# Two buffers of an fp32 transformer kernel placed 64 bytes later in SBUF

## The reference, cut to what matters

```
y = modulate(rmsnorm(h, norm), shift, scale)
h = h + 0.5 * gate * swiglu(y, w_gu, w_down)      # six times: 1024 -> 2 x 2816 -> 1024
q, k, v, gu, gv = split(y @ w_in)                  # block 1: attention and gMLP, then w_out
q, k, v, u = split(y @ even_in)                    # block 2, layer 0: attention and Hyena
q, k, v, g = split(y @ ret_in)                     # block 2, layer 1: retention
shift, scale, gate = split(silu(c) @ w_ada + b)    # nine vectors of 1024 for each layer
```

## Time and profile before

| | |
|---|---|
| median of three runs | 2521.0 us |
| the profiled execution, its own time | 2521.01 us |
| its span | 2518.8 us |
| TensorE busy | 2441.2 us, 97% of the span |
| VectorE busy | 1515.7 us, 60% |
| ScalarE busy | 893.0 us, 35% |
| mean granted TensorE clock | 0.983 |

### The profile page before, as it was taken

How to read it: one execution, slowest core, us unless ns; L and a number is a source line. 1 busy time by engine, 2 the same in 40 slices (tenths; PEclk the granted TensorE clock), 3 DMA queues, 4 the chain that set the end, 5 groups by cost and what they waited for, 6 DMA issues and landing times.

```text
span 2518.8 us, 39335 instructions
## 1 busy us (share of the span) xinstructions
PE 2441.2 (97%) x14736; PEld 2153.7 (86%) x14736; DVE 1515.7 (60%) x2434; ACT 893.0 (35%) x1103; POOL 380.4 (15%) x353
## 2 busy tenths in 40 slices
PE   6998989999999998999999999999999999999999
PEld 4998879999888888867788888888888889999999
DVE  7676767977877665356478776642222365555444
ACT  4443454454222223432232222242222242244443
POOL 2110531211111102332211111001110001000110
PEclk7999989999999999999999999999999999999999
DMA  7778736854655554211135555522222242134455
GB/s 278 277 261 278 256 134 213 272 198 165 220 187 188 174 167 144 80 63 51 67 115 201 195 169 186 167 87 97 100 84 92 91 160 72 64 117 167 170 177 169
DMA packets 79878, 400.19 MB, mean 159 GB/s; under 512 B 8816, under 2 KB 12912, under 8 KB 54704
## 3 DMA queue, kind: packets, MB, share of 16 engines
q1 hardware_dynamic: 77216, 393.39, 45.1%
q0 software_dynamic: 1056, 3.67, 0.4%
q10 hardware_dynamic: 1520, 1.95, 0.2%
HBM read 396.88 MB, written 2.10 MB: 158 GB/s over the span
## 4 chain that ended last, share of the span: by engine, by line
PE 83%; DVE 8%; ACT 3%; DMA 3%; issue 2%; POOL 0%; ACTq 0%; SPq 0%; DVEq 0%; POOLq 0%
PE pg L1158 24%; PE pg L1160 23%; PE pg L1159 23%; DMA raw<-w_d 2%; PE pg L1334 2%; PE pg L1335 2%; PE pg L1336 2%; DVE wlo L2048 1%; PE px L1976 1%; DMA raw<-w_t 1%; ACT whi L661 1%; DVE ada L2088 1%; PE px L1737 1%; ACT whi L666 1%; PE pg L1776 1%
## 5 line engine op out<-in xcount | busy, mean ns | idle before, releaser
L1158 PE MATMUL pg<-Yh,whi 128*128 128x256 f32 (+1 forms) x2856 | 957.4, 335 | 28.5 <-DVE Yl L2208 7.7
L1159 PE MATMUL pg<-Yl,whi 128*128 128x256 f32 (+1 forms) x2856 | 946.9, 332 | 0.0
L1160 PE MATMUL pg<-Yh,wlo 128*128 128x256 f32 (+1 forms) x2856 | 946.8, 331 | 0.0
L2053 DVE TENSOR_TENSOR wlo<-raw,whi 128x2048 fp32r<-128x2048 f32 (+1 forms) x202 | 415.3, 2056 | 517.3 <-ACT whi L666 516.5
L1158 PEld LDWEIGHTS pg<-Yh,whi 128*128 128x128 f32 x2856 | 546.6, 191 | 91.5 <-issue 21.0
L1160 PEld LDWEIGHTS pg<-Yh,wlo 128*128 128x128 f32 x2856 | 546.5, 191 | 49.9
L1159 PEld LDWEIGHTS pg<-Yl,whi 128*128 128x128 f32 x2856 | 546.8, 191 | 49.2
L666 ACT ACTIVATE whi<-raw 128x2048 fp32r<-128x2048 f32 (+1 forms) x202 | 348.4, 1725 | 565.0 <-PE pg L1160 517.2
L1158 PE MATMUL pg<-Hh,whi 128*128 128x256 f32 (+1 forms) x1122 | 367.1, 327 | 7.0 <-DVE wlo L2053 4.5
L1160 PE MATMUL pg<-Hh,wlo 128*128 128x256 f32 (+1 forms) x1122 | 364.9, 325 | 0.0
L1159 PE MATMUL pg<-Hl,whi 128*128 128x256 f32 (+1 forms) x1122 | 364.8, 325 | 0.0
(11 more groups left out here) (352 smaller groups left out, 2361.7 us busy)
## 6 DMA issues: line engine op xcount, KB each, us to landing
raw<-w_t SPq DMA_DIRECT2D x194, 1024.0 KB, 5.0
ada<-w_ada SPq DMA_DIRECT2D x200, 512.0 KB, 3.6
raw<-w_d SPq DMA_DIRECT2D x96, 704.0 KB, 4.1
ADA<-w_ada SPq DMA_DIRECT2D x16, 512.0 KB, 14.0
NB<-na_bias POOLq DMA_DIRECT2D x8, 256.0 KB, 2.9
X<-x_t ACTq DMA_DIRECT2D x2, 512.0 KB, 16.4
spectrum<-HF POOLq DMA_DIRECT2D x1, 1024.0 KB, 11.1
X<-ctx_t SPq DMA_DIRECT2D x1, 1024.0 KB, 8.1
```

Of the source, the lines that this page charges most:

```text
L1158: pe.matmul(out, w_hi, y_hi, start=first, stop=False)
L1159: pe.matmul(out, w_hi, y_lo, start=False, stop=False)
L1160: return pe.matmul(out, w_lo, y_hi, start=False, stop=last)
L2053: dve.tensor_tensor(wlo[:, n % 2, 0:size], raw[:, n % 2, 0:size], whi[:, n % 2, 0:size].bitcast(F32), ALU.subtract)\
```

## The change

```
     X = sb("X", [P, KD, 512])
+    at[0] += 64
     y_at = at[0]
     Yh = sb("Yh", [P, 4096], F32R)
     Yl = sb("Yl", [P, 4096], F32R)
+    at[0] += 64
     raw = sb("raw", [P, 2, BLK])
     whi = sb("whi", [P, 2, BLK], F32R)
     wlo = sb("wlo", [P, 2, BLK], F32R)
```

## The result

The changed kernel takes 2531.1 us, the median of seven runs (2524.9 to 2539.7), against 2520.3 for the kernel before (seven runs, 2517.2 to 2526.8). The ratio is 1.0043, with a 95% interval from 1.0028 to 1.0057: 10.8 us slower, 7 to 14. I had forecast 4.6 us faster, and the time lies above the range.

The account below looks back on a forecast made before the run. TensorE's matmul pace was taken to bound the kernel, busy 97% of the span. Terms -22.1 (256 columns), +23.9 (512 columns) and -6.4 (Y stationary) sum to -4.6 us, 2521.0 to 2516.4 us; range 2512 to 2529.5.

Parts of the forecast that it names:

- its two signs: Matmuls over moving Y: 256 columns get 6.67 ns shorter, 22.1 us gained; 512 columns 6.67 ns longer, 23.9 us lost.
- the rule of even and odd by 128 bytes: All float32r products: paces are even multiples of 16 cycles where both operands' remainders by 128 agree, odd where they differ.
- D: Rival: the remainder is not the cause, H's pace comes from something else in its stages, nothing moves, 2521.0 us; chance 0.06.
- The 512-column term: Moving Y at 512 columns, mainly l0_gu1, l0_gu2 and l1_gu1: each matmul 6.67 ns longer, 23.9 us lost in all.
- I take from the H rows that a matmul of 256 columns over a moving Y gets 6.67 ns shorter: Moving Y at 256 columns: pace goes from 120.0 to 113.3 ns, 22.1 us gained after what is hidden.
- I count both stages in full: b1_gu1 and l1_gu2: weights keep up, so all 1056 matmuls in each count, 7.04 us each, 14.1 us gained together.
- the matmuls with Y stationary: 960 matmuls in l0_in and l1_in: one step of 6.67 ns each, taken as a gain of 6.4 us.
- B: Rival: only the moving operand's place counts, matmuls with Y stationary keep 120.0 ns, 2522.8 us; chance 0.26.
- C: Rival: a stationary operand off the 128-byte mark is dearer, 126.7 ns in l0_in and l1_in, 2529.2 us; chance 0.14.
- my terms for the 512-column matmuls in `l0_in` and `l1_in`: Moving Y at 512 columns, partly hidden: 2.8 us lost from l0_in to l0_out and 1.1 us in l1_in.
- The stretches that I had set to nothing: b1_down1, b1_down2 and l1_down2 at 0; in b1_in no product leads the chain, so no gain was taken.
- `b1_gu2`: 256 columns over Y: VectorE's loop of 5.72 us a block makes TensorE wait for wlo, gain 2.1 us instead of 7.04.

Follow-up runs that it names:

- e2: Kernel before with weights' parts whi and wlo 64 bytes later and H, behind them, 128 later, Y unmoved; 2527.9 us, ratio 1.0020.
- e1: Changed kernel with whi and wlo also 64 bytes later and all behind them 128 later, so Y, weights and H have remainder 64; 2533.5 us, ratio 1.0045.
- e13: Kernel before with weights 64 bytes later in l0_gu2 and, behind two blocks, in l0_gu1 and l1_gu1 (512 columns); 2541.6 us, ratio 1.0086.
- e9: Kernel before with weights 64 bytes later only in b1_gu1, b1_out, b1_gu2 and l1_gu2 (256 columns); 2509.0 us, ratio 0.9950.
- e14: Kernel before with weights 64 bytes later only in the value blocks, those with Y stationary; ratio 0.9993.
- e4: The changed kernel again, word for word, for a second trace; 2531.6 us, ratio 1.0036 against the kernel before.
- e3: Kernel before with the region of H and OH moved to difference 0 from the weights; 2517.8 us, ratio 0.9979.
- e5: Kernel before with pads that put Y 64 bytes and H 32 bytes above the weights, by 256; ratio 0.9995.
- e7: Kernel before with pads that put Y 32 bytes and H 64 bytes above the weights, by 256; ratio 1.0029.
- e8: Kernel before with pads that put Y 32 bytes below and H 96 bytes above the weights, by 256; ratio 1.0079.
- e6: Kernel before with pads that put both Y and H 128 bytes from the weights, by 256; ratio 1.0090.
- e12: Kernel before with each weight block at its foreseen best place: difference 0 for 512 columns, moving 64 below stationary for 256; 2494.8 us, ratio 0.9902.

## Why the prediction was wrong, point by point

**The cause and its two signs were right, the rule behind them was not.** Y took over H's paces, 512 columns got dearer and 256 cheaper, and the two operands count against each other (e2). But the rule of even and odd by 128 bytes fell with e1. D, the case in which the remainder does nothing, is out: a shift of 64 bytes in the weights moved the time by 21.7 us in e13. The Trainium skill has lines of 16 bytes in "SBUF — State Buffer" (note on cachelines); by that a shift of whole lines would do nothing, and the measurement differs. What failed is the sum, which was a small difference of large terms, each with its own error.

**The 512-column term was right.** The three clean stages lost 7.2, 7.7 and 6.4 us where 6.6, 7.0 and 6.4 were foreseen, and by itself the part measures +21.7 us (e13) for a forecast of 20.0.

**The step that failed: "I take from the H rows that a matmul of 256 columns over a moving Y gets 6.67 ns shorter".** The one pair of rows that I read the earlier trace rows shows 113.3 ns. H had a second pace in the same trace, 117.8 ns in some 290 matmuls, which I had not looked for. Here it is in the kernel before, in `b1_down1`, 5.65 us for 48:

```profile
201.80 0.28 PE L1158 MATMUL pg<-Hh,whi 128*128 128x256 f32 x1
...
207.45 0.28 PE L1158 MATMUL pg<-Hh,whi 128*128 128x256 f32 x1
```

A third of the changed kernel's Y matmuls of 256 columns (some 1430 in streams long enough to tell) go at it and win 2.2 ns and not 6.67. That is 1430 x 4.4 ns, or 6.3 us of the 22.1. The part by itself gave -12.6 us (e9, -9.1 to -16.1), where my terms for its stages were 7.04 + 7.04 + 2.1 and about 0.9 for `b1_out`: 17.1. Beside the pace, "I count both stages in full" held for `l1_gu2` (-6.7) and not for `b1_gu1`, whose four stops, three of them behind late loads, took 1.8 us in the first trace.

**The second step: the matmuls with Y stationary.** "The rule of odd and even that fits all five paces" fitted five rows with two differences in them, and e1 broke it. The term was -6.4 us, and is -1.8 (e14): the moving operand lies 64 above the stationary one there, and not below as in the H rows, and the pace is 117.8 from end to end. Of the rivals, B (no gain there) came closest to this term. Its mechanism is wrong too, since by e2 the stationary operand's place counts as much as the moving one's. C, a dearer stationary operand, did not happen; its time of 2529.2 us was nearest to the measured one by chance.

**The rest.** The terms as measured apart are +21.7 (e13), -12.6 (e9) and -1.8 (e14). With my terms for the 512-column matmuls in `l0_in` and `l1_in` (+3.9), and leads and other 256-column parts at the 2.1 + 2.9 us that I gave them at most, that makes +6 to +11; the change measured +10.8 (7 to 14). Of the 15.4 us between forecast and result the three terms give 1.7, 4.5 and 4.6; the other 4.6 are not shown by any run. The stretches that I had set to nothing (`b1_in` with `b1_out` +2.1, `b1_down2` +0.9, `l1_down2` +1.8, `b1_down1` -1.4) add 3.4 us in the one pair of traces. In `l1_down2` and `b1_down2` this is H's draw between its two paces (in `b1_down2` some 330 steps at 117.8 after, 100 before). The others differ between two executions of the changed kernel too: `b1_down1` with its norm takes 78.4 us in the first trace and 81.3 in e4, and `b1_gu1` begins at 45.8 and 48.5. Their cause is not shown.

**`b1_gu2`** gained 1.6 us for a forecast of 2.1, and 2.3 in e4. VectorE's loop held TensorE there as forecast, with its terms a little off. This is the first trace, VectorE and then TensorE:

```profile
421.85 2.29 DVE L2055 TENSOR_TENSOR wlo<-raw,whi 128x2048 fp32r<-128x2048 f32 x1
...
427.54 2.28 DVE L2055 TENSOR_TENSOR wlo<-raw,whi 128x2048 fp32r<-128x2048 f32 x1
```

```profile
424.54 0.28 PE L1162 MATMUL pg<-Yh,wlo 128*128 128x256 f32 x1
424.65 0.33 PE L1160 MATMUL pg<-Yh,whi 128*128 128x256 f32 x1
424.82 0.28 PE L1161 MATMUL pg<-Yl,whi 128*128 128x256 f32 x1
```

The block starts 0.51 us after the subtraction's end at 424.14, its first step takes 0.17 instead of 0.11 us, and behind that the stream has turned to 117.8 ns. VectorE's turn is 5.69 us here and 5.59 in the one before, a mean of 5.64 where I had set 5.72. From there on, for most of the stage, TensorE takes 5.65 us a block at 117.8 ns, which is about the same: in this trace the slower pace and VectorE's loop give nearly one time, and the table cannot tell them apart. In e4 more blocks drew 113.3 ns, and 15 of the 21 blocks behind the first start within 0.6 us of a subtraction's end.

**The range** was built around the signs of one disputed term, and took the paces themselves as exact. A bound from the slower H pace in the trace (117.8 for all 256-column matmuls) would have given 2.2 instead of 6.67 ns, a third of 22.1 us, and with no gain for Y stationary 2521.0 - 7.4 + 23.9, some 2537 us, beyond my upper end.

## What to carry to other kernels

Where TensorE streams float32r without breaks, read the pace from start to start for each pair of buffers and each width, over whole stages and not at one place: equal instructions that run at several paces can mean that the place of the buffers counts. Here the difference of the two operands' starts by 256 bytes decides which paces occur; of the seven that were tried 0 is best for 512 columns and -64 for 256, and room of 256 bytes for each weight buffer with an offset for each block gave 1% without another instruction. When a change has a large term of either sign, the range must come from the bounds of both, not from their difference.

## What the runs showed of the hardware

- The paces of float32r matmuls with 128 stationary columns depend on where the moving operand starts relative to the stationary one, by 256 bytes: at 512 columns from 226.7 ns (0; Y before, H in e1, e2, e3) to 233.3 (-64; Y after), at 256 from 113.3 (-64; H before, Y after) to 120.0 (0). The unit is at most 32 bytes (e5, e7, e8).
- The sign counts: -64 and +64 give 233.3 and 228.8 ns at 512 columns (after; e5, e7).
- At some differences a stream has one of several paces: at 256 columns 113.3 or 117.8 ns at -64, 118.6 or 120.0 at 128 (e1, e6). It keeps one until the next break, and two executions of the same program differ in which (the changed kernel and e4).
- The best place for 512 columns (0) is at the slowest pace seen for 256, 120.0 ns, so that one layout for both widths gives part of one away (before; e12).
- From the end of a subtraction to the first matmul that waits for it, 0.51 us (the changed kernel, 424.65) and 0.58 us (e4, 438.54) went by.
